# Second attention of a fused two-layer block: the normalisation of the exponentials moves from a diagonal on TensorE to a scaling on GpSimd

## The reference, cut to what matters

```python
s_loc = jnp.einsum('bnqhd,binchd->bhnqic', qr, kb) * scale + bias
s_loc = jnp.where(mask, s_loc, NEG_INF)
s_ctx = jnp.einsum('bnqhd,bkhd->bhnqk', qr, k_ctx) * scale
sc = jnp.concatenate([s_loc, s_ctx], axis=-1)
p = jax.nn.softmax(sc, axis=-1)
o = einsum(p_loc, vb) + einsum(p_ctx, v_ctx)
```

## Time and profile before

| | us |
|---|---|
| median of three runs | 2614.68 |
| the profiled execution | 2613.15 |
| its span | 2611.4 |
| TensorE matmuls busy | 2431.6 (93%) |
| VectorE busy | 1130.7 (43%) |
| ScalarE busy | 786.5 (30%) |
| GpSimd busy | 738.3 (28%) |

### The profile page before, as it was taken

How to read it: one execution, slowest core, us unless ns; L and a number is a source line. 1 busy time by engine, 2 the same in 40 slices (tenths; PEclk the granted TensorE clock), 3 DMA queues, 4 the chain that set the end, 5 groups by cost and what they waited for, 6 DMA issues and landing times.

```text
span 2611.4 us, 32384 instructions
## 1 busy us (share of the span) xinstructions
PE 2431.6 (93%) x12062; PEld 2042.7 (78%) x12062; DVE 1130.7 (43%) x1397; ACT 786.5 (30%) x1077; POOL 738.3 (28%) x659
## 2 busy tenths in 40 slices
PE   4797999879999999999988989889999999999997
PEld 3586888767888888888777888879778888888885
DVE  7676888676441344124453351525221121222233
ACT  3226777203220122024424343434112111122210
POOL 1343222242333333323322111020213333333331
PEclk9898999998999999999998999999999999999998
DMA  5410000741111111111131101101001111111131
GB/s 224 169 44 33 16 16 25 275 152 40 48 48 44 47 48 49 47 65 46 36 117 39 69 19 50 52 16 63 32 28 48 48 48 52 48 48 40 48 121 72
DMA packets 45868, 165.49 MB, mean 63 GB/s; under 512 B 4208, under 2 KB 6000, under 8 KB 44656
## 3 DMA queue, kind: packets, MB, share of 16 engines
q1 hardware_dynamic: 45808, 164.67, 17.9%
HBM read 156.26 MB, written 8.39 MB: 63 GB/s over the span
## 4 chain that ended last, share of the span: by engine, by line
PE 84%; DVE 7%; ACT 3%; issue 3%; DMA 2%; POOL 1%; SPq 0%; DVEq 0%; ACTq 0%; POOLq 0%
PE acc L624 63%; PE bank L863 3%; PE turn L850 3%; PE bank L738 3%; PE turn L724 2%; PE acc L707 2%; PE bank L724 1%; DVE ADA L1310 1%; PE acc L836 1%; PE bank L579 1%; DMA WF<-in_w 1%; PE acc L592 1%; DVE K2L L1655 1%; DMA ADA<-in_ada 1%; PE bank L906 1%
## 5 line engine op out<-in xcount | busy, mean ns | idle before, releaser
L624 PE MATMUL acc<-HH,WH 128*128 128x512 f32 x1792 | 557.2, 392 | 11.0 <-POOL WL L499 10.5
L624 PE MATMUL acc<-HL,WH 128*128 128x512 f32 x1792 | 554.5, 391 | 0.0
L624 PE MATMUL acc<-HH,WL 128*128 128x512 f32 x1792 | 554.3, 391 | 0.0
L496 POOL TENSOR_TENSOR WH<-WF,CON 128x16 fp32r<-128x16 f32 x186 | 54.7, 294 | 1608.0 <-PE acc L624 1423.1
L499 POOL TENSOR_TENSOR WL<-WF,WH 128x1024 fp32r<-128x1024 f32 (+2 forms) x186 | 439.1, 2361 | 15.5
L624 PEld LDWEIGHTS acc<-HH,WH 128*128 128x128 f32 x1792 | 337.3, 189 | 83.8 <-POOL WL L499 9.3
L624 PEld LDWEIGHTS acc<-HL,WH 128*128 128x128 f32 x1792 | 338.2, 189 | 70.7
L624 PEld LDWEIGHTS acc<-HH,WL 128*128 128x128 f32 x1792 | 338.1, 189 | 70.8
L1568 DVE SCALAR_TENSOR_TENSOR CV<-EV,VEC,CV 128x1023 f32<-128x1023 f32 x44 | 106.2, 2414 | 245.5 <-ACT CV L1109 245.5
L497 POOL TENSOR_SCALAR WH<-WF 128x1008 fp32r<-128x1008 f32 (+2 forms) x186 | 187.0, 1005 | 0.0
L1509 DVE SCALAR_TENSOR_TENSOR XT<-acc,MOD,XT 128x1024 f32 (+1 forms) x40 | 51.2, 1282 | 245.8 <-PE acc L624 245.8
(11 more groups left out here) (302 smaller groups left out, 3798.6 us busy)
## 6 DMA issues: line engine op xcount, KB each, us to landing
WF<-in_w SPq DMA_DIRECT2D x150, 512.0 KB, 3.3
ADA<-in_ada SPq DMA_DIRECT2D x9, 2048.0 KB, 8.9
ADA<-in_ada SPq DMA_DIRECT2D x14, 1024.0 KB, 15.3
BIAS<-in_bias SPq DMA_DIRECT2D x8, 1152.0 KB, 5.1
XT<-in_xT SPq DMA_DIRECT2D x16, 512.0 KB, 9.8
WF<-in_w SPq DMA_DIRECT2D x24, 256.0 KB, 2.6
ADA<-in_ada SPq DMA_DIRECT2D x8, 512.0 KB, 3.3
out_xT<-XT SPq DMA_DIRECT2D x1, 4096.0 KB, 11.7
```

Source lines behind the costliest of these rows:

```text
L496: pool.tensor_tensor(h[:, 0:FEW], f[:, 0:FEW], zero.to_broadcast([P, FEW]), ALU.add).then_inc(w_hi, 1)
L624: last = pe.matmul(acc[:, slot, HALF * c:HALF * c + HALF], w[slot][:, k, :], x[:, k, HALF * c:HALF * c + HALF], start=(k == 0 and w is WH ...
```

## The change

GpSimd multiplies the exponentials of a unit by the reciprocals of their sums in place: 16 columns by a tensor_tensor, 624 by a tensor_scalar with the column of reciprocals and 1.0. TensorE then turns the five blocks by transposes with the constant identity. VectorE no longer makes the diagonal. On GpSimd the splits of the tiles n+4 and n+5 now stand after the scaling of unit 2 and of unit 8 of the pass; the loop over passes is written out for it, and what is left of the splits follows as before.

```diff
+            def normalise2(u0, u):
+                pool.wait_ge(rc_ready, u0 + (64 + u + 1))
+                x, r = EX2[u % 3], RC[:, u % 2:u % 2 + 1]
+                pool.tensor_tensor(x[:, 0:FEW], x[:, 0:FEW], r.to_broadcast([P, FEW]), ALU.mult).then_inc(exn2_ready, 1)
+                pool.tensor_scalar(x[:, FEW:], x[:, FEW:], r, 1.0, ALU.mult, ALU.mult).then_inc(exn2_ready, 1)
+            split_w(N_ATT2, 0, KD)
+            split_w(N_ATT2 + 1, 1, KD)
+            with pool.Fori(0, 4) as it:
+                n = it * 4 + N_ATT2
+                split_w(n + 2, 0, KD)
+                split_w(n + 3, 1, KD)
+                for u in range(16):
+                    normalise2(it * 16, u)
+                    if u == 2:
+                        split_w(n + 4, 0, KD)
+                    if u == 8:
+                        split_w(n + 5, 1, KD)
-            for n0, count, k1 in ((N_ATT2, 12, KD), (N_GF, 16, 4), ...
+            for n0, count, k1 in ((N_F + 2, 3, KD), (N_GF, 16, 4), ...
...
                 def turn_probs(u):
-                    pe.wait_ge(dg_ready, u0 + (u + 1))
+                    pe.wait_ge(exn2_ready, 2 * u0 + (2 * u + 2))
...
-                            mm = pe.matmul(turn[:, part_col(k):part_col(k) + P], EX2[u % 3][:, P * k:P * k + P], DG[u % 2][:, :],
-                                           start=True, stop=True)
+                            mm = pe.transpose(turn[:, part_col(k):part_col(k) + P], EX2[u % 3][:, P * k:P * k + P], ident)
...
-                def diagonal(u):
+                def invert_sums(u):
                     dve.wait_ge(exp2_done, u0 + (u + 1))
                     dve.reciprocal(RC[:, u % 2:u % 2 + 1], SUM[:, u % 2:u % 2 + 1]).then_inc(rc_ready, 1)
-                    dve.wait_ge(rc_ready, u0 + (64 + u + 1))
-                    dve.tensor_scalar(DG[u % 2][:, :], ident, RC[:, u % 2:u % 2 + 1], None, ALU.mult).then_inc(dg_ready, 1)
```

More of the change, by code:

```diff
@@ L296, in build @@
         vt2_done, vtok2_ready = sem("vt2_done"), sem("vtok2_ready")
-        scores2_done, nb2_ready, exp2_done, dg_ready, pt2_done, pt2_ready, pv2_done, o2_ready = (
-            sem("scores2_done"), sem("nb2_ready"), sem("exp2_done"), sem("dg_ready"), sem("pt2_done"), sem("pt2_ready"),
+        scores2_done, nb2_ready, exp2_done, exn2_ready, pt2_done, pt2_ready, pv2_done, o2_ready = (
+            sem("scores2_done"), sem("nb2_ready"), sem("exp2_done"), sem("exn2_ready"), sem("pt2_done"), sem("pt2_ready"),
             sem("pv2_done"), sem("o2_ready"))
@@ L566, in _ @@
                         split_w(it * 2 + (N_DOWN[g] + s), s, gk)
-            for n0, count, k1 in ((N_ATT2, 12, KD), (N_GF, 16, 4), (N_A, 8, KD), (N_GA, 8, 4), (N_OUT2, 4, KD)):
+            def normalise2(u0, u):
[15 more added lines that the diff above has]
+                        split_w(n + 5, 1, KD)
+            for n0, count, k1 in ((N_F + 2, 3, KD), (N_GF, 16, 4), (N_A, 8, KD), (N_GA, 8, 4), (N_OUT2, 4, KD)):
                 with pool.Fori(0, count) as it:
@@ L1660, in _ @@
                 for u in range(16):
-                    diagonal(u)
+                    invert_sums(u)
                     if u < 14:
```

## The result

The changed kernel takes 2584.8 us (median of four runs, 2583.78 to 2585.47), the kernel before 2614.48 in four runs; the ratio is 0.9889, with a 95% interval of 0.9876 to 0.9902. The profiled execution took 2583.78 us, its span is 2582.0.

The account below looks back on a forecast made before the run. TensorE was taken as the bound inside a pass (50.0 of 52.3 us). Gains of 3.2 + 6.1 + 1.0 minus 4.4 a pass, 23.6 over four, minus 10.2 for the clock, gave 13.4: 2601 us, range 2588 to 2622.

Parts of the forecast that it names:

- The turn: TensorE in each unit of the second attention: five transposes at 0.11 us, 0.55 us instead of 1.12.
- that rival: TensorE's clock does not rise in the loop because of the transposes: a pass loses 27 us, 2720 us; chance 0.02.
- The period: Steady state, turn to turn: 2.31 us instead of 2.82, set by values waiting for the copy; 6.1 us a pass gained.
- The scaling: GpSimd scaling 624 columns in each unit: 0.71 us, ready in time for the turn with 0.15 us of slack.
- slow scaling: Rival: GpSimd scales at its two-input pace, 1.51 us for 624 columns, period 2.96; 2640 us, slower than before; chance 0.12.
- The head: Start of a pass: subtractions freed of the splits, first scores 2.9 us earlier; 3.2 us a pass gained, bounds 2.0 and 4.5.
- The tail: Last units of a pass, without scores: way through the copy 1.18 us instead of 1.52; 1.0 us a pass gained.
- The stalls: Whole splits in GpSimd's queue delay turns of units 3 and 9 by 2.2 us each: 4.4 us a pass lost.
- The clock behind the stalls: TensorE's clock falls to 0.66 for 5.0 us after six of eight stalls, 1.7 us each: 10.2 us lost.
- the clock that stays up: Rival: TensorE's clock does not fall after the short stalls; gain 23.6 us, up to 28, 2590 us; chance 0.22.
- the middling scaling: Rival: GpSimd's 624 columns take 0.94 us (first case, 2606) or 1.2 us (second, 2622); middle 2612 us; chance 0.15.

Follow-up runs that it names:

- the runs with another cut of the turn: The changed kernel with splits cut in three pieces, and the turn copied in parts of two and three blocks instead of three and two: 2564.81 us, ratio 0.9814.
- the kernel with the pieces: The changed kernel with each split in the loop cut in three, behind the scalings of units 2, 3, 4 and 8, 9, 10: 2571.34 us, on another chip 2569.89.
- the run with 1.23 us: The changed kernel with splits cut in three, its 624 columns scaled by GpSimd's two-input form with reciprocals broadcast: 2580.26 us, ratio 0.9874.
- the splits alone: The kernel before with the two splits moved into the loop at the same places and the diagonal kept: 2599.15 us against 2613.67, ratio 0.9947.
- the turn alone: The changed kernel with both splits put back in the head of the pass: 2585.98 us, ratio 0.9898 against the kernel before.
- the longer stalls: The changed kernel with one, two, three or five extra GpSimd operations behind each split in the loop: 2598.63, 2601.93, 2602.20 and 2616.27 us.

## Why the prediction was right and wrong

The direction held, and so did the mechanism of each term but one; the forecast was 16 us too high, and 10.2 of these are that one term, falls of TensorE's clock that did not occur.

1. **The turn.** Five records at 0.11 us and 0.55 us for the turn, as forecast. The Trainium skill says that TensorE's transpose mode "doesn't count as PE-busy the same way" (TensorE: Matmul & The Clock Gate, PE-mode transpose); here the clock was 1.00 in units with 0.55 us of transposes in each 2.29, so that rival fell; the low stretches in the passes are at their heads, as before the change.
2. **The period.** 2.31 forecast from the way through the copy, 2.29 measured (2.35 in the first pass); the runs with another cut of the turn showed that it was this chain. In the first pass the values start 0.60 us after the copy starts, and not 0.54: that is the 0.06 more. Twelve intervals, seen without stalls in the kernel with the pieces, gained 5.7 us in the first pass (33.87 to 28.17) and 6.4 in the others, 6.2 as a mean; 6.1 were forecast.
3. **The scaling.** 0.79 us instead of 0.71 for the 624 columns, behind 0.20 for the first 16. The middling and the slow scaling (0.94 and more) did not come, and the run with 1.23 us shows that even then the kernel, its splits in pieces, is ahead of before. The estimate of 0.94 us, worked out from the rate in the Trainium skill (GPSIMD Engine Reference, Elementwise — side-by-side cycle accounting), was too high by a fifth, and mine too low by a tenth.
4. **The head.** 3.2 us a pass forecast, 3.8 measured as a mean (15.05, 15.22, 15.42 and 15.52 us before from the last product to turn(1), 11.24, 11.52, 11.89 and 11.43 after). The wait before the scores came out at 2.88 us, as worked out. Between the first scores and turn(1) I had 0.3 (0.4 lost by the scaling, 1.1 gained by the turn of unit 0, 0.4 taken off for the clock), and 0.9 were measured: turn(0) came 0.6 later behind scores(2), and turn(1) 0.9 sooner behind turn(0), which together is what I had; but scores(2) came 0.58 us sooner behind the first scores. I had left the clock at 1.2 GHz for all of the head. In the kernel before it fell 1.0 to 1.9 us ahead of the first scores, in the changed one 0.9 to 2.3 us after them, so the scores of units 0 and 1 ran almost wholly at 2.4 GHz. The two runs with one half of the change each show that this is the move's: 3.27 us with the splits alone, 3.84 with the turn alone.
5. **The tail.** 1.0 us a pass forecast, 1.0 measured (8.9 to 7.9).
6. **The stalls.** Two a pass, at u = 3 and 9, ended by GpSimd, as forecast. 4.6 us from the end of scaling(2) to turn(3) was right (4.61). The slack that I set against it was not: scaling(2) lay 0.37 us ahead of its turn, not 0.15, so a stall is 1.95 us and not 2.2. That is 2 us over the eight.
7. **The clock behind the stalls: the step that failed.** I charged six falls of 1.7 us, 10.2 in all, from what followed the idle stretches in the middle of projections. There was none in eight stalls, and the kernel with the pieces shows it from the other side: without the stalls the passes are 15.4 us shorter, which is 8 x 1.95 alone. The size of a single fall was nearly right (1.5 us, seen in the longer stalls); their number was not. The fault is that I set two different measures side by side: 2.2 us was a distance from turn to turn less its period, and the 2.24 us of the earlier trace rows an idle time between records. In that second measure these stalls are 1.5 to 1.7 us, and of 76 single idle stretches of 1.3 to 1.7 us that began at full clock in the thirteen profiled executions (these eight among them) one was followed by a fall within 5 us. That the shorter idle time was the whole reason is not shown: 1.95 us of stall, lengthened to an idle time of 2.0 to 2.4 us, brought one fall in eight in one execution and by the times more in the others.

The sum with the measured terms: 3.8 + 6.2 + 1.0 - 3.9 = 7.1 a pass, 28.4 for four, against 29.0 from the passes' lengths and 29.7 from the medians. The 16.2 us between forecast and result are thus 10.2 of the clock, 2.4 of the heads, 2.0 of the stalls, 0.4 of the period, and 1.2 outside these terms. The nearest rival, the clock that stays up, had it right in kind and gave 2590: it lacked the 0.6 at each head and the 0.25 at each stall. The range was too narrow on this side: this rival's own upper gain of 28 us gives 2587, already below the 2588 at which the range began. Small slips in the working changed nothing of this: the second case of the middling scaling gains 2.0 us in its intervals and not 1.9, the middle of its two cases is 2614 and not 2612, and the chances of a time under 2609.5 add up to 0.76 and not 0.74.

What stays open: what decides whether the clock falls behind a wait. Of the idle stretches of 2.15 to 2.30 us outside the units that began at full clock, in the thirteen profiled executions, 47 of 62 were followed by a fall; at the place of the earlier trace rows at 1284 ten in ten, at the one at 1272 three in thirteen. In the units, in one profiled execution for each length, it fell once in eight at 2.0 to 2.4 us, three times in eight at 2.5 to 2.7, never in eight at 3.0 to 3.2 and eight times in eight at 3.9 to 4.2. And it fell behind much shorter waits too: at the transposes of the values TensorE waits 1.11 us twice, 2.2 us apart, and behind this pair the clock fell at 17 of 39 places in passes two to four of the thirteen executions, never in that of the kernel before and once in that of the changed kernel, where the window behind it has 0.67. What lies around a stretch must count beside its length; the runs do not say what.

```profile
1694.56 1.09 PE L834 MATMUL turn<-CON,VT 128*128 128x128 f32 x8 [1.11 <-ACT VTOK L1174]
1696.77 0.69 PE L834 MATMUL turn<-CON,VT 128*128 128x128 f32 x2 [1.11 <-ACT VTOK L1174]
```

```profile
1696.80:1701.80 5.00, 5.00 (x28) 4.96 (x29) 0.56 (x1) 3.69 (x6) 0.00 (x0) 0.67 0.32 105
```

## What to carry to other kernels

An operation that is put in front of the bounding engine's next input costs its whole length less the slack there, so a long one is cut into pieces no longer than the idle time of the engine that does it: here that was worth 13.5 us, as much as the move itself. Before a penalty is charged for an idle stretch, it and the stretch that it is compared with are to be taken in the same measure, and the penalty is to be seen in a row for a stretch of this length in such surroundings; if no row shows it, it belongs in the range and not in the sum. And when the bound falls, the second chain is worked out at once: cutting the turn into two and three blocks, a change of two lines, brought the period to TensorE's own work and with the tails 5.1 us.

## What the runs showed of the hardware

- GpSimd's multiplication by a column of scalars takes 0.79 us for 128 x 624 float32 and 1.11 us for 128 x 1008, a little more than the form with two constants (1.03 us for 1008); with the scalar broadcast as a second tensor it is 1.23 us for 624, and with two true tensors 2.36 us for 1024.
- Beside VectorE's operations on the scores, which have an operand in PSUM, GpSimd's scaling was never stretched (0.785 to 0.799 us in all 64 units), whereas two operations with all operands in SBUF had stretched each other in the earlier trace rows.
- A float32 transpose of 128 x 128 goes through TensorE once, in 0.11 us; the product with a diagonal went twice, in 0.22.
- In the first of the four passes the period was 2.35 us and in the other three 2.29, with three and two blocks; with two and three it was 2.26 in all four. The 0.06 lie between the start of ScalarE's copy and that of the values; why they do, nothing here shows.
